# Scaled residual of two layer norms: one VectorE instruction reading PSUM in place of a TensorE product and a ScalarE copy

## The chip, the core and the metric

The kernel runs on one core of a Trainium2 chip. A core has five engines that run side by side and meet only at semaphores: TensorE (PE, matrix products into PSUM), VectorE (DVE), ScalarE (ACT), GpSimd (POOL) and SyncE (SP), which here issues loads. The metric is the device time of one execution in microseconds (us).

## What is computed

One decoder layer over 2048 tokens of width 1024. The change touches the two places at which a residual, scaled by ALPHA = 2 ** 0.25, is added ahead of a layer norm:

```python
mix = jnp.einsum('ble,ed->bld', jnp.concatenate([pool_out, attn_out], axis=-1), w_out[l])
h = layer_norm(ALPHA_RES * h + mix, ln1_g[l], ln1_b[l])
ffn = moe(h, w_router[l], b_router[l], w_gate_up[l], b_gate_up[l], w_down[l], b_down[l])
h = layer_norm(ALPHA_RES * h + ffn, ln2_g[l], ln2_b[l])
```

Everything is float32. Attention picks 256 keys per query by an index score; the mixture of experts takes the best 4 of 32 experts for every token.

## The kernel before

The tokens are cut into 16 blocks of 128. The program has five stages, one after the other: input projection (to about 600 us), attention (to about 2290 us), the placing of tokens to experts, the experts' products (to about 5607 us) and combine (to the end).

**Attention** (`attend_stage`). Each engine runs its own list of work in an order that the function `walk` writes out by hand, and the engines meet by counted semaphores. Round b of the walk handles six heads of block b, the search for the 256 best keys of block b+1 (VectorE, cut into six parts by `parts`), the index scores of block b+2 (`score`, up to four pieces), and the end of block b-1: output projection (`project`), statistics, norm, transposes, routing. The beginning of a round reads:

```python
piece("logits", b, 0)
piece("choose", b - 2)
search(b + 1, 0)
fill(b, 0, ("project", b - 1))
piece("logits", b, 1)
search(b + 1, 1)
fill(b, 1, ("score", b + 2, 0))
```

An engine skips the pieces for which it has no function. `project` on TensorE first claims the PSUM tile `pair` (two banks of 512 columns), then for each bank multiplies eight slices of `mixT` by `w_out` (L936) and adds a ninth product, `alpha_ident` (ALPHA times the identity) by `h` (L938). ScalarE's `project` copies `pair` into the tile `res` (L1039) and raises the semaphore `s_res`. VectorE's `statistics` (L776, L777), two pieces of the walk further on, waits for `s_res`; and so does TensorE's `claim` before whatever uses `pair` next: in rounds 1 to 13 that is the first product of `score(b+2, 0)` (L855), in later rounds another piece. The logits row maximum of VectorE is L756, its search rows are L725 to L730, TensorE's logits L876 and L878, its sum of the normalised diagonals L904.

**Combine** (`combine_stage`). For each block t, with two slots in turn: GpSimd makes four diagonal matrices of the gates (L1639) and gathers the rows of four experts (L1644); TensorE adds `alpha_ident` by `h1` (L1687), the gathered rows by the diagonals (L1692), in the middle of which it transposes the gate sums by expert (L1697) that VectorE made (L1716), and the bias product (L1702); ScalarE copies the sum to `total` (L1749); VectorE takes statistics (L1724 to L1729), GpSimd the power (L1651), VectorE scales (L1733, L1736), GpSimd adds the bias (L1655), ScalarE issues the store (L1753). VectorE's order within a block is gate sums, statistics, scaling. GpSimd's order is power(t), gather(t+2), bias(t). The load of `h1` for block t+1 is issued by SyncE once the product sum of block t-1 is done (`s_sum`).

Of the kernel before, what the change touches and what calls it, by code (L numbers as in the profile page):

```python
# [67 lines left out]
def wait(eng, sem, value):  # L68

    if not isinstance(value, int) or value > 0:  # L70
        eng.wait_ge(sem, value)
# [306 lines left out]
def attend_stage(nc, A, S, D_):  # L378
# [84 lines left out]
    with ExitStack() as ctx:  # L463
        def sb(name, shape, dt=F32):
            return ctx.enter_context(nc.sbuf_tensor(name, shape, dt))
# [27 lines left out]
        h1 = res  # L493
        h1T = h[:].rearrange("p (k n) -> p k n", n=P)
        ident_bf = sb("ident_bf", [P, P], BF16)
        alpha_ident = sb("alpha_ident", [P, P])
        ones = sb("ones", [P, P])
        before = sb("before", [P, P])
        expert_no = sb("expert_no", [P, EXPERTS])
# [73 lines left out]
        with nc.Block() as block:  # L573
# [57 lines left out]
            def _(pool):  # L631
# [7 lines left out]
                nc.gpsimd.iota(expert_no[:], pattern=[[1, EXPERTS]], base=0, channel_multiplier=0,  # L639
                               allow_small_or_imprecise_dtypes=True)  # L640
                nc.gpsimd.iota(token[:], pattern=[[P, TILES]], base=0, channel_multiplier=1)
                nc.gpsimd.tensor_copy(ident_bf[:], S["ident"][:])
                nc.gpsimd.tensor_scalar(alpha_ident[:], S["ident"][:], ALPHA_RES, 1.0, ALU.mult, ALU.mult
                                        ).then_inc(s_made, 1)
                pool.drain()
                pool.wait_ge(s_made, 2)
                nc.gpsimd.affine_select(out=before[:], in_=before[:], compare_op=ALU.is_gt, fill=0.0,
# [66 lines left out]
            def _(dve):  # L714
# [53 lines left out]
                def inverse(b, g):  # L768
# [2 lines left out]
                    nc.vector.reciprocal(inv_sum[:, g * REP:(g + 1) * REP], sums[:, g * REP:(g + 1) * REP]  # L771
                                         ).then_inc(s_inv, 1)

                def statistics(b):
                    dve.wait_ge(s_res, b + 1)
                    nc.vector.bn_stats(stats[:, 0:6], res[:, 0:512])  # L776
                    nc.vector.bn_stats(stats[:, 6:12], res[:, 512:1024])  # L777
                    dve.drain()
                    wait(dve, s_norm, b)
                    nc.vector.bn_aggr(mean_var, stats)  # L780
                    dve.drain()
                    nc.vector.tensor_scalar(var_eps, mean_var[:, 1:2], EPS, None, ALU.add).then_inc(s_var, 1)
# [22 lines left out]
                def weigh(b):  # L805
# [17 lines left out]
                dve.wait_ge(s_const, CONSTS)  # L823
                dve.wait_ge(s_made, 4)
                walk({"logits": logits, "inverse": inverse, "choose": choose, "search": search_part, "select": select,
                      "statistics": statistics, "weigh": weigh})

            @block.tensor
            def _(pe):
# [99 lines left out]
                def project(b, head):  # L929
                    claim(*PAIR)  # L930
                    pe.wait_ge(s_mix, KV * (b + 1))
                    pe.wait_ge(s_pools, b + 1)
                    pe.wait_ge(s_hl, 16 * (b + 1))
                    for n in range(2):
                        for k in range(KD):
                            nc.tensor.matmul(pair[:, n], mixT[:, k], w_out[:, k, n * BANK:(n + 1) * BANK],  # L936
                                             start=(k == 0), stop=False)
                        op = nc.tensor.matmul(pair[:, n], alpha_ident[:], h[:, n * BANK:(n + 1) * BANK],  # L938
                                              start=False, stop=True)
                    op.then_inc(s_out, 1)  # L940
                    used["res"] = b + 1

# [31 lines left out]
            def _(act):  # L974
# [58 lines left out]
                def project(b, head):  # L1033
                    if head:
                        exp(*head)
                    act.wait_ge(s_out, b + 1)
                    wait(act, s_h1st, 16 * b)
                    wait(act, s_ht, 2 * b)
                    nc.scalar.activation(res[:], pair[:].rearrange("p a b -> p (a b)"), ACT.Copy).then_inc(s_res, 1)  # L1039

                def norm(b):
                    act.wait_ge(s_rstd, b + 1)
# [512 lines left out]
def combine_stage(nc, A, S, D_):  # L1555


    with ExitStack() as ctx:
# [10 lines left out]
        g_now = sb("g_now", [P, TOP_E])  # L1569
        rows = sb("rows", [P, 2, TOP_E, D])  # L1570
        h1 = sb("h1_blk", [P, 2, D])
        alpha_ident = sb("alpha_ident2", [P, P])
        g_diag = sb("g_diag", [P, 2, TOP_E, P])
        by_pick = sb("by_pick", [P, TOP_E, EXPERTS])
        by_expert = sb("by_expert", [P, 2, EXPERTS])
# [36 lines left out]
        with nc.Block() as block:  # L1612
            @block.sync
            def _(sp):
                sp.dma_start(b_down[:], A["b_down"][0]).then_inc(s_const, 16)
                sp.dma_start(gain[:], A["ln2_g"][0].partition_broadcast(P)).then_inc(s_const, 16)
                sp.dma_start(bias[:], A["ln2_b"][0].partition_broadcast(P)).then_inc(s_const, 16)

                def body(t, slot, half):
                    wait(sp, s_sum, t - 1)  # L1620
                    sp.dma_start(h1[:, slot], D_["h1"][cut(t), :]).then_inc(s_h1[slot], 16)

                pairs(sp, body)

            @block.gpsimd
            def _(pool):
                nc.gpsimd.tensor_scalar(alpha_ident[:], S["ident"][:], ALPHA_RES, 1.0, ALU.mult, ALU.mult
                                        ).then_inc(s_made, 1)
                nc.gpsimd.memset(minus_half[:], -0.5).then_inc(s_made, 1)

                def gather(t, slot, half):
                    wait(pool, s_sum, t - 1)
                    if not isinstance(t, int) or t >= 2:
                        pool.wait_ge(s_rows[slot], 64 * half)
                    nc.gpsimd.tensor_copy(at[:, slot], S["pos"][:, t])
                    nc.gpsimd.tensor_copy(g_now[:], S["gates"][:, t])  # L1636
                    pool.drain()  # L1637
                    for k in range(TOP_E):
                        op = nc.gpsimd.tensor_scalar(g_diag[:, slot, k], S["ident"][:], g_now[:, k:k + 1], 1.0,  # L1639
                                                     ALU.mult, ALU.mult)  # L1640
                    op.then_inc(s_gd, 1)
                    pool.drain()  # L1642
                    for k in range(TOP_E):
                        nc.gpsimd.indirect_dma_start(  # L1644
                            rows[:, slot, k], None, D_["y"], bass.IndirectOffsetOnAxis(ap=at[:, slot, k:k + 1], axis=0)
                        ).then_inc(s_rows[slot], 16)

                def power(t, slot):
                    var_eps, rstd = small[:, slot, 14:15], small[:, slot, 15:16]
                    pool.wait_ge(s_var, t + 1)  # L1650
                    nc.gpsimd.tensor_tensor(rstd, var_eps, minus_half[:], ALU.pow).then_inc(s_rstd, 1)  # L1651

                def finish(t, slot):
                    pool.wait_ge(s_norm, t + 1)
                    nc.gpsimd.tensor_tensor(out[:, slot], out[:, slot], bias[:], ALU.add).then_inc(s_out, 1)  # L1655

                pool.wait_ge(s_made, 2)
                pool.wait_ge(s_const, 48)
                gather(0, 0, 0)
                gather(1, 1, 0)  # L1660

                def body(t, slot, half):
                    power(t, slot)
                    gather(t + 2, slot, half + 1)
                    finish(t, slot)

                for t in range(4):
                    body(t, t % 2, t // 2)
                with pool.Fori(2, TILES // 2 - 1) as i:
                    body(2 * i, 0, i)  # L1670
                    body(2 * i + 1, 1, i)
                for t in (TILES - 2, TILES - 1):
                    power(t, t % 2)
                    finish(t, t % 2)

            @block.tensor
            def _(pe):
                pe.wait_ge(s_const, 48)
                pe.wait_ge(s_made, 2)

                def body(t, slot, half):
                    pe.wait_ge(s_h1[slot], 16 * (half + 1))
                    wait(pe, s_tot, t - 1)
                    pe.wait_ge(s_gd, t + 1)
                    for n in range(2):
                        cols = slice(n * BANK, (n + 1) * BANK)
                        nc.tensor.matmul(acc[:, slot, cols], alpha_ident[:], h1[:, slot, cols], start=True, stop=False)  # L1687
                    pe.wait_ge(s_rows[slot], 64 * (half + 1))
                    for n in range(2):
                        cols = slice(n * BANK, (n + 1) * BANK)  # L1690
                        for k in range(TOP_E):
                            nc.tensor.matmul(acc[:, slot, cols], g_diag[:, slot, k], rows[:, slot, k, cols],  # L1692
                                             start=False, stop=False)
                        if n == 0:
                            pe.wait_ge(s_by, t + 1)
                            wait(pe, s_bts, t)
# [12 lines left out]
            def _(dve):  # L1709
# [9 lines left out]
                def body(t, slot, half):  # L1719
                    gates(t, slot)  # L1720
                    stats, mean_var = small[:, slot, 0:12], small[:, slot, 12:14]
                    var_eps, rstd = small[:, slot, 14:15], small[:, slot, 15:16]
                    dve.wait_ge(s_tot, t + 1)
                    nc.vector.bn_stats(stats[:, 0:6], total[:, slot, 0:512])  # L1724
                    nc.vector.bn_stats(stats[:, 6:12], total[:, slot, 512:1024])
                    dve.drain()
# [15 lines left out]
            def _(act):  # L1742
                def body(t, slot, half):
                    act.wait_ge(s_bt, t + 1)
                    wait(act, s_sum, t)
                    nc.scalar.activation(by_expertT[:], trp[0:EXPERTS, 0:P], ACT.Copy).then_inc(s_bts, 1)
                    act.wait_ge(s_sum, t + 1)
                    wait(act, s_norm, t - 1)
                    nc.scalar.activation(total[:, slot], acc[:, slot], ACT.Copy).then_inc(s_tot, 1)  # L1749

                def store(t, slot):
                    act.wait_ge(s_out, t + 1)
# [83 lines left out]
```

## Time and profile before

| | |
|---|---|
| Three runs | 5859.07, 5876.14, 5882.66 us, median 5876.14 |
| Profiled execution, its span | 5876.0 us (no other time of it is listed) |
| TensorE busy | 5062.7 us, 86% |
| VectorE busy | 3078.1 us, 52% |
| ScalarE busy | 1843.3 us, 31% |
| GpSimd busy | 977.3 us, 17% |
| Mean granted TensorE clock | 0.930 of full speed |

The span is the time from the first to the last instruction of one profiled execution. Busy shares are means over stages with different limits. A row names the line, the engine and operation, then what is written and read, with the tile's size; "idle before <- X" is the time in which the engine stood still ahead of the instruction and what ended it. "PEld" is the loading of weights, which overlaps the products.

### The profile page before, as it was taken

The numbers are of one execution on the slowest core, as the hardware profiler recorded it, in microseconds if no ns is written. First come the engines' busy times: TensorE is split into PE (matmuls) and PEld (weight loads), VectorE is DVE, ScalarE is ACT, GpSimd is POOL, SyncE is SP. The second block draws the span as 40 slices with busy tenths as digits, with TensorE's granted clock in tenths as the row PEclk, the third lists the DMA queues.
The fourth block names the chain that finished last, engine by engine and source line by source line (L and its number), as shares of the span: only waits on it lengthen the run. The fifth ranks groups of instructions, "written<-read, shape, count | busy, mean of one in ns | idle before, by whom it ended". The sixth has DMA issues, their size and how long they took to land. (4 is left out here: it accounts for less than half of the span.)

```text
span 5876.0 us, 68835 instructions
## 1 busy us (share of the span) xinstructions
PE 5062.7 (86%) x23758; PEld 3683.0 (63%) x23759; DVE 3078.1 (52%) x4877; ACT 1843.3 (31%) x2663; POOL 977.3 (17%) x1073
## 2 busy tenths in 40 slices
PE   7998788999999864889888889889888989898977
PEld 3444343444444432878887888788878878788832
DVE  2121467788777753644445444554555455544522
ACT  1111223333333321433333333333343333433310
POOL 0000122111111111211111111111111111111145
PEclk9999789999999986999999999999999999999988
DMA  5232110001000002544444543544454444544455
GB/s 189 103 115 100 45 24 17 20 16 20 12 12 10 14 8 70 184 159 152 137 160 156 170 138 130 181 138 159 164 176 138 150 167 152 183 160 137 138 178 184
DMA packets 427127, 670.22 MB, mean 114 GB/s; under 512 B 22064, under 2 KB 286256, under 8 KB 425552
## 3 DMA queue, kind: packets, MB, share of 16 engines
q1 hardware_dynamic: 367776, 507.46, 26.4%
q0 software_dynamic: 26576, 85.56, 4.1%
q10 hardware_dynamic: 32256, 69.22, 3.1%
q8 instruction: 456, 7.47, 0.5%
q14 instruction: 63, 0.52, 0.0%
HBM read 542.86 MB, written 119.31 MB: 113 GB/s over the span
## 5 line engine op out<-in xcount | busy, mean ns | idle before, releaser
L1352 PE MATMUL gu<-x_hi,w_hi 128*128 128x256 f32 (+2 forms) x4096 | 1292.6, 316 | 313.8 <-issue 218.7
L1354 PE MATMUL gu<-x_hi,w_lo 128*128 128x256 f32 (+2 forms) x4096 | 1277.6, 312 | 10.9 <-issue 10.9
L1353 PE MATMUL gu<-x_lo,w_hi 128*128 128x256 f32 (+2 forms) x4096 | 1279.0, 312 | 2.4 <-issue 2.4
L1419 DVE TENSOR_TENSOR w_lo<-w_raw,w_hi 128x2048 fp32r<-128x2048 f32 x386 | 874.7, 2287 | 529.1 <-ACT w_hi L1493 529.1
L1352 PEld LDWEIGHTS gu<-x_hi,w_hi 128*128 128x128 f32 x4096 | 820.9, 200 | 339.4 <-issue 294.5
L1493 ACT ACTIVATE w_hi<-w_raw 128x2048 fp32r<-128x2048 f32 x386 | 726.1, 1905 | 375.9 <-PE gu L1354 290.9
L1354 PEld LDWEIGHTS gu<-x_hi,w_lo 128*128 128x128 f32 x4096 | 818.4, 200 | 14.6 <-issue 14.6
L1353 PEld LDWEIGHTS gu<-x_lo,w_hi 128*128 128x128 f32 x4096 | 820.3, 200 | 0.0
L1325 POOL TENSOR_TENSOR a_lo<-up,a_hi 128x384 fp32r<-128x384 f32 x256 | 395.7, 1546 | 1965.0 <-ACT a_hi L1505 1965.0
L1430 DVE TENSOR_SCALAR gate<-gu,b_gu 128x384 f32<-128x384 f32 x256 | 158.1, 617 | 829.2 <-PE gu L1354 829.2
L1352 PE MATMUL yp<-w_hi,a_hi 128*128 128x512 f32 x1296 | 536.5, 414 | 0.0
L1353 PE MATMUL yp<-w_lo,a_hi 128*128 128x512 f32 x1296 | 523.5, 404 | 0.0
L1354 PE MATMUL yp<-w_hi,a_lo 128*128 128x512 f32 x1296 | 522.9, 403 | 0.0
L298 PE MATMUL proj_acc<-w_in_sb,hT 128*128 128x512 f32 (+1 forms) x1280 | 474.0, 531 | 7.1 <-DMA w_in_sb<-w_in 5.0
L298 PEld LDWEIGHTS proj_acc<-w_in_sb,hT 128*128 128x128 f32 x1280 | 225.3, 191 | 255.8 <-issue 249.3
L725 DVE TENSOR_SCALAR_CACHE_REDUCE mask<-scores_odd,small 128x512 bf16<-128x512 f32 (+6 forms) x224 | 346.0, 1545 | 18.7 <-issue 1.6
L1501 ACT ACTIVATE sig<-gate 128x384 f32<-128x384 f32 x256 | 132.7, 518 | 686.9 <-DVE gate L1430 686.9
L725 DVE TENSOR_SCALAR_CACHE_REDUCE mask<-scores_even,small 128x384 bf16<-128x384 f32 (+6 forms) x224 | 316.1, 1411 | 18.2 <-issue 0.7
L860 PE MATMUL acc<-relu,w_diag 128*128 128x512 f32 (+3 forms) x608 | 304.9, 600 | 0.6 <-ACT relu L983 0.3
L876 PE MATMUL qk<-kT,q_blk 128*128 128x512 f32 (+3 forms) x480 | 235.1, 574 | 79.0 <-ACT probs L998 58.4
L855 PE MATMUL pair<-ikT,iq_blk 64*128 64x512 f32 (+3 forms) x608 | 277.3, 601 | 25.1 <-ACT relu L983 23.7
L756 DVE TENSOR_REDUCE small<-qk 128x1 f32<-128x128 f32 (+15 forms) x96 | 124.0, 1291 | 324.1 <-PE qk L878 286.3
(256 smaller groups left out, 5940.2 us busy)
## 6 DMA issues: line engine op xcount, KB each, us to landing
w_raw<-w_gate_up SPq DMA_DIRECT2D x258, 1024.0 KB, 7.6
w_raw<-w_down SPq DMA_DIRECT2D x128, 1024.0 KB, 7.1
y_dram<-y_rows ACTq DMA_DIRECT2D x192, 256.0 KB, 2.9
y_dram<-zeros SPq DMA_DIRECT2D x16, 2016.0 KB
h_blk<-h_dram SPq DMA_DIRECT2D x32, 512.0 KB, 6.5
qi_dram<-qi_stage ACTq DMA_DIRECT2D x16, 640.0 KB, 2.9
w_in_sb<-w_in SPq DMA_DIRECT2D x1, 8480.0 KB, 23.7
x_in<-x SPq DMA_DIRECT2D x16, 512.0 KB, 9.2
```

Of the source, the lines that this page charges most:

```text
L298: mm = nc.tensor.matmul(acc[:, n, 0:width], hT[:, slot, k], w_in[:, k, c0:c0 + width], start=(k == 0), stop=(k == KD - 1))
L725: nc.vector.tensor_scalar(reach, s, limit, 0.0, ALU.is_ge, ALU.add, accum_out=n_reach)
L855: nc.tensor.matmul(pair[:, (u0 + i) % 2, 0:width], iq[row, b % 2, i // 2], S["ikT"][row, at:at + width], start=True, stop=True).then_inc(s ...
L860: nc.tensor.matmul(acc[:, 0:width], w_diag[:, j], relu[:, (u0 + j) % 2, 0:width], start=(j == 0), stop=(j == IDX_H - 1)).then_inc(s_wsum, 1)
L876: nc.tensor.matmul(qk[:, at:at + width], q[:, b % 2, i], S["kT"][:, i // REP, at:at + width], start=True, stop=False)
L1325: nc.gpsimd.tensor_tensor(a_lo[:, j], up[:, j % 2], a_hi[:, j].bitcast(F32), ALU.subtract).then_inc(s_al, 1)
L1352: nc.tensor.matmul(out, s_hi_, m_hi, start=(n == 0), stop=False)
L1353: nc.tensor.matmul(out, s_hi_, m_lo, start=False, stop=False)
L1354: op = nc.tensor.matmul(out, s_lo_, m_hi, start=False, stop=(n == len(pairs) - 1))
L1419: nc.vector.tensor_tensor(w_lo[:, c % 2, cols], raw[:, c % 3, cols], w_hi[:, c % 2, cols].bitcast(F32), ALU.subtract).then_inc(s_lo, 1)
L1430: nc.vector.tensor_scalar(g, gu[:, j % 2, 0, 0:ROWS], S["b_gu"][:, j, bass.ds(e, 1)], LIMIT, ALU.add, ALU.min).then_inc(s_gm, 1)
L1493: nc.scalar.activation(w_hi[:, c % 2, cols], raw[:, c % 3, cols], ACT.Copy).then_inc(s_hi, 1)
```

## The change

In attention, VectorE gets a piece `project` that computes `res = ALPHA * h + pair` in one instruction out of PSUM and raises `s_res`; the ninth product and ScalarE's copy go; the wait for `h` moves from TensorE to VectorE. In combine, VectorE computes `total = ALPHA * h1 + acc` and raises `s_tot` before it takes the statistics; the product L1687 and the copy L1749 go; SyncE's load of `h1` waits for `s_tot` in place of `s_sum`. The search parts are cut as before.

```diff
+                def residual(b, head):
+                    dve.wait_ge(s_out, b + 1)
+                    dve.wait_ge(s_hl, 16 * (b + 1))
+                    wait(dve, s_h1st, 16 * b)
+                    wait(dve, s_ht, 2 * b)
+                    nc.vector.scalar_tensor_tensor(res[:], h[:], ALPHA_RES, pair[:].rearrange("p a b -> p (a b)"),
+                                                   ALU.mult, ALU.add).then_inc(s_res, 1)
                 def statistics(b):
-                    dve.wait_ge(s_res, b + 1)
+                    dve.drain()
...
-                      "statistics": statistics, "weigh": weigh})
+                      "project": residual, "statistics": statistics, "weigh": weigh})
...
-                    pe.wait_ge(s_hl, 16 * (b + 1))
                     for n in range(2):
                         for k in range(KD):
-                            nc.tensor.matmul(pair[:, n], mixT[:, k], w_out[:, k, n * BANK:(n + 1) * BANK],
-                                             start=(k == 0), stop=False)
-                        op = nc.tensor.matmul(pair[:, n], alpha_ident[:], h[:, n * BANK:(n + 1) * BANK],
-                                              start=False, stop=True)
+                            op = nc.tensor.matmul(pair[:, n], mixT[:, k], w_out[:, k, n * BANK:(n + 1) * BANK],
+                                                  start=(k == 0), stop=(k == KD - 1))
...
-                    act.wait_ge(s_out, b + 1)
-                    wait(act, s_h1st, 16 * b)
-                    wait(act, s_ht, 2 * b)
-                    nc.scalar.activation(res[:], pair[:].rearrange("p a b -> p (a b)"), ACT.Copy).then_inc(s_res, 1)
...
-                    wait(sp, s_sum, t - 1)
+                    wait(sp, s_tot, t - 1)
...
-                    pe.wait_ge(s_h1[slot], 16 * (half + 1))
                     wait(pe, s_tot, t - 1)
                     pe.wait_ge(s_gd, t + 1)
-                    for n in range(2):
-                        cols = slice(n * BANK, (n + 1) * BANK)
-                        nc.tensor.matmul(acc[:, slot, cols], alpha_ident[:], h1[:, slot, cols], start=True, stop=False)
...
-                    dve.wait_ge(s_tot, t + 1)
+                    dve.wait_ge(s_sum, t + 1)
+                    dve.wait_ge(s_h1[slot], 16 * (half + 1))
+                    nc.vector.scalar_tensor_tensor(total[:, slot], h1[:, slot], ALPHA_RES, acc[:, slot],
+                                                   ALU.mult, ALU.add).then_inc(s_tot, 1)
+                    dve.drain()
...
-                    act.wait_ge(s_sum, t + 1)
-                    wait(act, s_norm, t - 1)
-                    nc.scalar.activation(total[:, slot], acc[:, slot], ACT.Copy).then_inc(s_tot, 1)
```

GpSimd no longer makes the two `alpha_ident` tiles.

## Rows read from the trace of the kernel before

**Rows 1.** The page: the span.

```profile
span 5876.0 us, 68835 instructions
```

**Rows 2.** Stretches by stage: busy us of PE, PEld, DVE, ACT, POOL, granted clock, DMA share, GB/s.

```profile
640.00:2330.00 1690.00, 1441.05 (x4640) 677.59 (x4638) 1225.58 (x2466) 519.15 (x1003) 285.28 (x395) 0.93 0.07 16
...
5608.00:5876.00 268.00, 191.34 (x400) 74.50 (x400) 68.45 (x128) 20.64 (x32) 143.94 (x192) 0.86 0.58 192
```

**Rows 3.** Waits in attention: who waited for whom, us in total, times, longest.

```profile
DVE small L756 <- PE qk L878: 252.4, 54, 18.4
...
PE pair L904 <- POOL r_diag L673: 40.1, 14, 9.5
```

**Rows 4.** Timeline of round 12: start us, us, engine, line, operation.

```profile
1716.25 1.89 DVE L756 TENSOR_REDUCE small<-qk 128x1 f32<-128x1664 f32 x1 [10.09 <-PE qk L878]
...
1730.70 1.02 PE L938 MATMUL pair<-h_blk,alpha_ident 128*128 128x512 f32 x2
...
1731.56 1.02 PE L876 MATMUL qk<-kT,q_blk 128*128 128x512 f32 x2
...
1735.15 1.13 PE L855 MATMUL pair<-ikT,iq_blk 64*128 64x512 f32 x4
...
1736.61 1.89 DVE L756 TENSOR_REDUCE small<-qk 128x1 f32<-128x1664 f32 x1
```

**Rows 5.** Timeline of rounds 1 and 13, the same places.

```profile
660.38 1.02 ACT L1039 ACTIVATE res<-pair 128x1024 f32<-128x1024 f32 x1 [17.05 <-PE pair L938]
661.61 1.13 PE L855 MATMUL pair<-ikT,iq_blk 64*128 64x512 f32 x4 [0.73 <-issue]
661.87 0.42 DVE L756 TENSOR_REDUCE small<-qk 128x1 f32<-128x256 f32 x1
...
1874.19 1.13 PE L855 MATMUL pair<-ikT,iq_blk 64*128 64x512 f32 x4
1874.29 2.02 DVE L756 TENSOR_REDUCE small<-qk 128x1 f32<-128x1792 f32 x1 [0.49 <-PE qk L878]
```

**Rows 6.** Groups by form: busy us, mean ns of one; VectorE, and ScalarE's and GpSimd's.

```profile
L739 DVE SCALAR_TENSOR_TENSOR scores_odd<-scores_odd,small,mask 128x1024 f32<-128x1024 f32 x1 | 1.3, 1285 | 0.1
L756 DVE TENSOR_REDUCE small<-qk 128x1 f32<-128x1024 f32 x6 | 7.3, 1225 | 8.7 <-PE qk L878 8.5
L1749 ACT ACTIVATE total<-c_acc 128x1024 f32<-128x1024 f32 x16 | 16.4, 1024 | 81.7 <-PE c_acc L1702 81.7
L1655 POOL TENSOR_TENSOR out_blk<-out_blk,bias 128x1024 f32<-128x1024 f32 x16 | 37.7, 2355 | 4.9 <-DVE out_blk L1736 4.6
```

**Rows 7.** Timeline of rounds 14 and 15.

```profile
2029.91 2.16 DVE L756 TENSOR_REDUCE small<-qk 128x1 f32<-128x1920 f32 x1
2034.34 2.08 PE L876 MATMUL qk<-kT,q_blk 128*128 128x512 f32 x2 [16.10 <-ACT probs L998]
...
2164.20 2.29 DVE L756 TENSOR_REDUCE small<-qk 128x1 f32<-128x2048 f32 x1 [15.33 <-PE qk L878]
```

**Rows 8.** Stretches at and behind gaps of TensorE, columns as in rows 2.

```profile
2041.00:2045.40 4.40, 0.00 (x0) 0.00 (x0) 4.17 (x7) 1.95 (x2) 0.23 (x1) 1.00 0.00 0
2045.40:2050.00 4.60, 4.58 (x8) 1.90 (x9) 2.33 (x4) 1.24 (x1) 2.60 (x4) 0.63 0.02 4
...
2179.70:2185.00 5.30, 5.25 (x7) 2.15 (x8) 0.00 (x0) 1.24 (x2) 3.15 (x5) 0.50 0.00 0
...
1848.00:1856.00 8.00, 6.16 (x19) 2.89 (x18) 0.92 (x1) 0.98 (x2) 2.06 (x4) 1.00 0.01 2
...
5749.70:5754.90 5.20, 5.13 (x10) 2.29 (x11) 0.00 (x0) 0.00 (x0) 3.43 (x6) 0.71 0.22 48
```

**Rows 9.** Timeline of combine.

```profile
5729.53 1.02 ACT L1749 ACTIVATE total<-c_acc 128x1024 f32<-128x1024 f32 x1 [5.16 <-PE c_acc L1702]
...
5735.98 0.28 PE L1697 MATMUL c_tr<-ident,by_expert 128*32 128x128 f32 x1 [1.22 <-DVE by_expert L1716]
...
5750.06 1.42 POOL L1639 TENSOR_SCALAR g_diag<-ident,g_now 128x128 f32<-128x128 f32 x4 [4.62 <-issue]
```

More of the change, by code:

```diff
@@ L495, in attend_stage @@
         ident_bf = sb("ident_bf", [P, P], BF16)
-        alpha_ident = sb("alpha_ident", [P, P])
         ones = sb("ones", [P, P])
@@ L641, in _ @@
                 nc.gpsimd.iota(token[:], pattern=[[P, TILES]], base=0, channel_multiplier=1)
-                nc.gpsimd.tensor_copy(ident_bf[:], S["ident"][:])
-                nc.gpsimd.tensor_scalar(alpha_ident[:], S["ident"][:], ALPHA_RES, 1.0, ALU.mult, ALU.mult
-                                        ).then_inc(s_made, 1)
+                nc.gpsimd.tensor_copy(ident_bf[:], S["ident"][:]).then_inc(s_made, 1)
                 pool.drain()
@@ L1571, in combine_stage @@
         h1 = sb("h1_blk", [P, 2, D])
-        alpha_ident = sb("alpha_ident2", [P, P])
         g_diag = sb("g_diag", [P, 2, TOP_E, P])
@@ L1626, in _ @@
             def _(pool):
-                nc.gpsimd.tensor_scalar(alpha_ident[:], S["ident"][:], ALPHA_RES, 1.0, ALU.mult, ALU.mult
-                                        ).then_inc(s_made, 1)
                 nc.gpsimd.memset(minus_half[:], -0.5).then_inc(s_made, 1)
@@ L1655, in finish @@
                     nc.gpsimd.tensor_tensor(out[:, slot], out[:, slot], bias[:], ALU.add).then_inc(s_out, 1)
-                pool.wait_ge(s_made, 2)
+                pool.wait_ge(s_made, 1)
                 pool.wait_ge(s_const, 48)
@@ L1678, in _ @@
                 pe.wait_ge(s_const, 48)
-                pe.wait_ge(s_made, 2)
                 def body(t, slot, half):
-                    pe.wait_ge(s_h1[slot], 16 * (half + 1))
                     wait(pe, s_tot, t - 1)
                     pe.wait_ge(s_gd, t + 1)
-                    for n in range(2):
-                        cols = slice(n * BANK, (n + 1) * BANK)
-                        nc.tensor.matmul(acc[:, slot, cols], alpha_ident[:], h1[:, slot, cols], start=True, stop=False)
                     pe.wait_ge(s_rows[slot], 64 * (half + 1))
@@ L1692, in body @@
                             nc.tensor.matmul(acc[:, slot, cols], g_diag[:, slot, k], rows[:, slot, k, cols],
-                                             start=False, stop=False)
+                                             start=(k == 0), stop=False)
                         if n == 0:
```

## The prediction

> **What bounds the kernel now.** I read the busy shares first, then the stretches by stage, then the waits of each changed stage, then the timeline around the changed instructions. The page gives a span of 5876.0 us [rows 1]. The stretches put the change's first half (attention, 640 to 2330 us) in a stretch with TensorE busy 1441 of 1690 us and VectorE 1226, and its second half (combine, 5608 to 5876 us) in one where no engine is busy all the time and DMA moves 192 GB/s [rows 2]. The 3278 us of expert work between them are not touched and I charge nothing there. In attention the waits say who is late: VectorE waits 252 us, in 54 waits, for TensorE's rows of logits, so TensorE is the bound and VectorE has room on average [rows 3]; ScalarE, idle 17 us before its first copy [rows 5], arrives early at the work that it gives away. The average is the trap: what counts is where VectorE is at the moment at which the new instruction stands in its queue.
>
> **Where the new instruction stands.** For round b of the walk, VectorE's order becomes logits(b,0), choose(b-2), first part of the search, *residual(b-1)*, logits(b,1). TensorE's order is logits(b,0), project(b-1), logits(b,1), score(b+2,0), and score claims the PSUM tile "pair", that is, it waits for the semaphore that ScalarE's copy raised and VectorE's sum will raise. Round 12 [rows 4]: the last alpha product begins at 1730.70, TensorE goes on with logits at 1731.56 and starts the score at 1735.15. VectorE is in its search until 1736.6 (its next row starts at 1736.61 with no idle before it), so the sum can't start before 1736.6, some 5 us after the projection is done.
>
> **Sum for rounds 1 to 13 (those with a score piece).** Let S be the start of the first score product (L855) and D the start of VectorE's second logits row (L756), which is when VectorE is free. D minus S is, round by round: 0.26, 2.08, 2.90, 2.08, 1.60, 1.03, 2.58, 0.97, 2.17, 0.19, 0.86, 1.46, -0.32 (13 rounds; the first, twelfth and last in [rows 4, 5]; in round 13 VectorE idles 0.49 before its row, so D there is 1873.87, the end of the search plus the usual 0.07). Together 17.9 us over 13 rounds. After the change the score starts at D + duration of the sum + hop to TensorE.
> - Duration: not in the trace. Nearest from below is ScalarE's 128x1024 copy out of PSUM, 1.024 us; from above the same kind of VectorE instruction with all operands in SBUF, 1.285 us; VectorE's own 1024-wide read of PSUM takes 1.225 [rows 6]. I take 1.25, nearest to the last two. An upper end far away is GpSimd's 1024-wide addition, 2.35 us, if the two should hold each other up.
> - Hop: in round 1 the copy starts at 660.38, takes 1.02, and the score, which waited for it, starts at 661.61: 0.21 us [rows 5].
> So 17.9 + 13 x 1.46 = +36.8 us. The saving on TensorE does not offset this: the two alpha products cost 0.86 us of its time each (1730.70 to 1731.56 [rows 4]), 1.72 us per block, but in these rounds they only make TensorE wait 1.72 us longer. After the score has started, everything in the round is paced by TensorE: VectorE's next logits row again begins with a wait for TensorE, and so does the first row of the next round (10.09 us in round 12 [rows 4]). So I carry the whole delay through, and VectorE's own 1.3 us are hidden in those waits.
>
> **Rounds 14 to 16.** Round 14 has no score piece; TensorE there waits 16.1 us for VectorE's logits row at 2029.91, so VectorE's 1.25 + 0.07 count: +1.3. Round 15: VectorE idles 15.3 us at that place, the sum lies in the idle time, TensorE's 1.72 come through: -1.7. Round 16 (last projection): -1.7, then 1.25 and a drain of 0.1 in place of the copy's 1.02 and its hand-over: -1.4 [rows 5, 7]. Together -1.8.
>
> **The clock.** The new wait is a gap on TensorE between the end of logits(b,1), now 1.72 earlier, and the new start of the score: 2.8 to 6.3 us, twelve of the thirteen over 3. Gaps in the trace show what follows: behind 4.4 us without a product the granted clock was 0.63 over the next 4.6 us, in another place 0.50 over 5.3 us, in combine 0.71 over 5.2 us, while around a gap of 1.84 us it stayed at 1.00 [rows 8]. The engine has two levels, 2.4 and 1.2 GHz, so these are 1.7, 2.6 and 1.5 us of work lost. The score piece is not pure TensorE time (ScalarE's part lies between its products), so I take 1.5 a round, twelve rounds: +18. Bounds: 0, if the level falls only inside the gap, and 2.6 x 13 = 34.
> The Trainium skill ("TensorE: Matmul & The Clock Gate", section "HAM oscillation — how this bites in real kernels") describes a loop whose every step waits for data between products and therefore begins every step at the lower clock. The rows agree; by the rule every round would pay, as in my sum; without it the sum would be 18 us smaller.
>
> **Combine.** The gather of one slot goes in a circle: last product of tile A (ends 5729.4), ScalarE's copy from 5729.53 to 5730.55, statistics, GpSimd's power, diagonals and four gathers, rows landed, products again at 5749.7 [rows 8, 9]. From the end of the product to the statistics it is 0.11 + 1.02 + 0.03 = 1.16 us now; after it 0.1 + 1.25 + 0.07 = 1.42 or, with the instruction at 1.285, 1.45: +0.29. The other tile, B, gets its end from VectorE's by_expert through the transpose (1.22 us idle at 5735.98 [rows 9]), which comes 0.29 later too. Seven turns, the last B tile and the last norm: 9 x 0.29 = +2.6. The alpha products (L1687, 1.7 us) lie in front of a wait for gathered rows or of that transpose; taking them away only lengthens a wait. The load of h1 is now issued after the sum, about 1.3 us later: it is wanted only by VectorE a tile later, and leaves the gather's transfers a little more room at first; at most 1.35 us of its 512 KB over 7.6 us, some 90 KB, or 0.4 us a turn. I take +2 for the stage, between -1 and +2.6 (up to +12 if tile B, too, were to start at the lower clock and it mattered; it waits for the other tile's rows 4.6 us anyway, at L1639 [rows 9]).
> GpSimd's alpha_ident in both stages (0.3 us each) lies before waits for loads: 0.
>
> **Sum.** 36.8 - 1.8 + 18 + 2 = +55 us on the profiled execution's span of 5876.0 us. No other time of that execution is given; the median of the three runs is 5876.14, so both give **5931 us**.
>
> **Rivals.**
> 1. *The wait without the clock*: as above, but the lower level falls in the gaps. For it: the gap of 1.84 us, behind which the clock stayed at 1.00. Against it: the three low rows in [rows 8]. 5876 + 37 = 5913 us.
> 2. *The delay is taken up later*: the late score shortens waits that TensorE now has for GpSimd's diagonals (40 us, 14 waits [rows 3]) or ScalarE. Only VectorE's 1.3 us x 14 would come through: 5876 + 18 + 2 = 5896. Against: what GpSimd does there comes after TensorE's own score piece, so it moves along.
> 3. *TensorE's saving comes through* (other side): if VectorE reached the sum before the projection was done and the sum ended before logits(b,1), 3.5 us in round 12, the score would start 1.72 earlier: 16 x -1.72 + 2 = -25.5, 5850 us. It decides from D at least 1.5 + 1.7 us earlier than S; only in round 15 is that so, in the other rounds D is at best 0.3 us before S. VectorE's start is tied to TensorE by the logits row of the same round, so a faster TensorE doesn't bring it there.
> 4. *The sum is dearer on VectorE*, towards 2.35 us: 1.1 x 14 more, 5948 us. Against: VectorE's reads of PSUM at the same place run at 1.2 ns an element.
>
> **Chances.** Forecast 0.62 (own range 5917 to 5948), rival 1 0.16, 2 0.09, 3 0.04, 4 0.07, the rest 0.02. Range for eight in ten: 5900 to 5955; its low end takes rival 1 with a cheaper sum (1.02 us), its high end rival 4 or a clock loss near its bound. Half a per cent, about what a measurement of this kernel tells from no change, is 29 us: faster 0.03 (rival 3 with a quick run), same 0.13 (rival 2, the rest of 3, the edge of 1), slower 0.84.
>
> **What would show it.** In the changed profile: the first L855 product of rounds 1 to 13 waits for VectorE, starting about 1.5 us after the search's last row, with gaps of 3 to 6 us (some 60 us of idle in all); the sum lasts 1.2 to 1.3 us; attention is longer by about 53 us, combine by 2, experts by nothing. Granted clock right behind those gaps: 0.5 to 0.7 for some 3 us; if 1.0, rival 1. If the gaps are there and the stage is not longer, rival 2. It is all wrong if L855 does not wait.

## The result and the profile after

The changed kernel is slower: 5963.48 us median (5955.01 to 5970.09) against 5867.6 (5855.55 to 5882.66), ratio 1.015, 95% interval 1.0124 to 1.0177. The forecast of 5931 us had the sign, but its range (5900 to 5955) ends below the time. The profiled execution spans 5953.4 us, 77.4 more than that of before; split at the first instruction of the placing stage's TensorE work (attention ends there) and at the last of the experts stage, it gives three differences, and the forecast has none of them to size:

| us | before | after | difference | forecast |
|---|---|---|---|---|
| up to the end of attention | 2294.2 | 2495.8 | +201.6 | +53 |
| placing and experts | 3312.8 | 3195.7 | -117.1 | 0 |
| combine | 269.0 | 261.9 | -7.1 | +2 |

Stretches of the changed kernel, columns as in [rows 2] (busy us of PE, PEld, DVE, ACT, POOL, granted clock, DMA share, GB/s); the line for before is the first in [rows 2], with a clock of 0.93:

```profile
640.00:2495.80 1855.80, 1580.86 (x4558) 704.39 (x4557) 1216.00 (x2446) 503.07 (x986) 286.34 (x392) 0.84 0.05 14
...
2495.80:5691.50 3195.70, 2823.83 (x17046) 2610.70 (x17046) 1682.32 (x1966) 1196.80 (x1356) 526.93 (x425) 0.95 0.48 161
5691.50:5953.40 261.90, 180.01 (x336) 70.20 (x336) 88.63 (x144) 4.48 (x17) 150.82 (x193) 0.79 0.58 197
```

TensorE is busy *more* in attention (1581 us, before 1441) although 32 products (64 records in the trace) were taken from it: it works at a lower clock. And the experts stage, whose code was not touched, has a higher clock (0.95, before 0.93) and is shorter. Round 12 of the walk, which answers to [rows 4]:

```profile
1907.97 0.22 PE L883 MATMUL qk<-mask,ident_bf 128*128 128x128 bf16 x1
1911.72 1.22 DVE L776 SCALAR_TENSOR_TENSOR res<-h_blk,pair 128x1024 f32<-128x1024 f32 x1 [0.24 <-issue]
1912.86 1.88 DVE L753 TENSOR_REDUCE small<-qk 128x1 f32<-128x1664 f32 x1
1913.15 1.80 PE L860 MATMUL pair<-ikT,iq_blk 64*128 64x512 f32 x4 [4.96 <-issue]
...
1921.57 2.07 PE L865 MATMUL acc<-relu,w_diag 128*128 128x512 f32 x2
1923.58 2.07 PE L860 MATMUL pair<-ikT,iq_blk 64*128 64x512 f32 x2
...
1935.60 2.07 PE L860 MATMUL pair<-ikT,iq_blk 64*128 64x512 f32 x2
```

The first lines are as forecast: the search ends, VectorE's sum starts, the score starts 1.43 us after the sum's start, behind a gap of 4.96 us. The later ones are not: pairs of products of the score piece take 2.07 us and not 1.12, and they still do at 1935.6, 22 us after the gap. The granted clock of this round, in the changed kernel and then in the kernel before:

```profile
1908.00:1913.00 5.00, 0.19 (x3) 0.00 (x0) 4.37 (x10) 0.00 (x0) 0.00 (x0) 1.00 0.00 0
1913.00:1940.00 27.00, 26.23 (x29) 7.00 (x30) 14.13 (x22) 5.94 (x10) 0.00 (x0) 0.51 0.00 0
1940.00:2045.00 105.00, 96.59 (x334) 45.05 (x333) 76.00 (x113) 39.87 (x76) 23.95 (x27) 0.97 0.04 14
```

```profile
1735.00:1752.20 17.20, 15.87 (x35) 4.53 (x32) 15.45 (x25) 6.80 (x12) 0.00 (x0) 1.00 0.01 1
1752.20:1855.00 102.80, 96.57 (x339) 45.87 (x340) 76.15 (x114) 38.85 (x74) 23.95 (x27) 0.98 0.04 15
```

During the gap the clock is still 1.00; then it is at the lower level (1.2 GHz) to the last products of the score piece, and comes back at 1940.8, while six full-height records of L865 run without a pause. The length of the score piece over the rounds, from the first score product to the next work on TensorE (L966, L968 after): 17.1 us in each of rounds 2 to 13 before, 28.3 to 30.7 after.

| sums over the rounds | forecast | measured |
|---|---|---|
| later start of the score (after VectorE's row of logits), rounds 1 to 13 | +36.8 | +37.9 |
| longer score piece, rounds 2 to 13 (by the clock) | +18 for all | +151.9 |
| rest of rounds 2 to 12 | 0 | +2.0 |

Round 1, which has no rank work to mark the end of the piece, comes to +15.1 in all. Rounds 14 to 16, from one projection's start to the next, come to +2.0, -2.0 and -3.8.

### The profile page after: what moved, and what is told of

Read it like the earlier page. It is cut to its first block and busy times, and to the rows that moved or that the text cites. A ratio compares the mean times of both kernels' runs of the same rounds, so it can differ in the third digit from the quotient of the medians.

```text
span 5953.4 us, 68604 instructions
## 1 busy us (share of the span) xinstructions
PE 5138.7 (86%) x23630; PEld 3661.1 (61%) x23631; DVE 3114.4 (52%) x4909; ACT 1810.8 (30%) x2631; POOL 987.0 (17%) x1071
## 5 line engine op out<-in xcount | busy, mean ns | idle before, releaser
L1350 PE MATMUL yp<-w_hi,a_hi 128*128 128x512 f32 x1296 | 524.3, 405 | 0.0
L860 PE MATMUL pair<-ikT,iq_blk 64*128 64x512 f32 (+3 forms) x608 | 359.2, 756 | 84.8 <-issue 61.5
L985 ACT ACTIVATE relu<-pair 128x512 f32<-128x512 f32 (+3 forms) x304 | 161.0, 543 | 774.7 <-PE acc L865 434.3
L865 PE MATMUL acc<-relu,w_diag 128*128 128x512 f32 (+3 forms) x608 | 386.2, 743 | 1.8 <-ACT relu L985 1.6
```

The lines of the kernel that those rows point to most:

```text
L860: nc.tensor.matmul(pair[:, (u0 + i) % 2, 0:width], iq[row, b % 2, i // 2], S["ikT"][row, at:at + width], start=True, stop=True).then_inc(s ...
L865: nc.tensor.matmul(acc[:, 0:width], w_diag[:, j], relu[:, (u0 + j) % 2, 0:width], start=(j == 0), stop=(j == IDX_H - 1)).then_inc(s_wsum, 1)
L985: nc.scalar.activation(relu[:, (u0 + i) % 2, 0:width], pair[:, (u0 + i) % 2, 0:width], ACT.Relu).then_inc(s_relu, 1)
L1350: nc.tensor.matmul(out, s_hi_, m_hi, start=(n == 0), stop=False)
```

## The experiments

Each kernel was compared with the kernel before on the same chip. Stage times are of its profiled execution.

| kernel | ratio (95%) | to the end of attention | placing and experts | combine | instruction packets |
|---|---|---|---|---|---|
| before | 1 | 2294.2 | 3312.8 | 269.0 | 456 |
| the change | 1.015 (1.0124 to 1.0177) | 2495.8 | 3195.7 | 261.9 | 425 |
| e1_attend_only | 1.016 (1.0132 to 1.0188) | 2493.9 | 3198.2 | 270.5 | 426 |
| e2_combine_only | 0.9983 (0.9968 to 0.9998) | 2301.4 | 3298.9 | 264.1 | 456 |
| e3_filler | 0.9908 (0.9876 to 0.994) | 2340.1 | 3215.3 | 261.7 | 426 |
| e4_early | 0.9777 (0.9748 to 0.9806) | 2278.1 | 3192.7 | 261.1 | 425 |
| e5_padded | 0.9984 (0.9972 to 0.9995) | 2300.6 | 3293.8 | 260.4 | 456 |
| e6_before_moved | 1.0004 (0.9993 to 1.0014) | 2311.3 | 3311.6 | 270.5 | 456 |
| e7_late_load | 0.999 (0.9976 to 1.0004) | 2291.9 | 3311.2 | 266.3 | 456 |
| e8_wake | 1.0193 (1.0161 to 1.0225) | 2425.5 | 3285.6 | 262.7 | 444 |
| e9_before_shifted | 0.9827 (0.981 to 0.9843) | 2299.4 | 3195.9 | 270.1 | 427 |
| e10_keep_products | 0.9978 (0.9963 to 0.9993) | 2289.3 | 3299.8 | 259.0 | 456 |

**Each half alone.** e1 is the change in `attend_stage` on the old `combine_stage`, e2 the other way round; the edits are the parts of the diff.

```diff
 # e1: attend_stage as changed, combine_stage as before
 # e2: combine_stage as changed, attend_stage as before
```

> Only the attention half of the change. The changed kernel's attention stage was 202 us longer, its experts stage 115 us shorter, its combine 7 us shorter. Theory A (the clock stays low): behind the new wait of 3 to 6 us TensorE runs the whole score piece at 1.2 GHz, some 11 us a round; attention here ends at about 2490 us, as in the changed kernel, and the granted clock in the score piece behind the wait is 0.50. Theory B (my forecast's, the delay and some 1.5 us of clock a round): attention +53 us. Experts: if the shorter stage comes from what stands before it in TensorE's program, it is shorter by 115 us here too; if it comes from the combine half, it is as before. With A and the first: about 5965 us.

> Only the combine half of the change. Attention as before (ends at about 2290 us). Theory (circle of the gather with a dearer VectorE part): combine +2.6 us. Rival (something in combine gets shorter that I did not see, the load of h1 behind the sum or the products that are gone): combine -7 us, as in the changed kernel. Experts as before, if its 115 us come from the program ahead of it; 115 us shorter, if not.

The attention half carries both large effects: attention to 2493.9 us and experts at 3198.2. The combine half leaves both (2301.4, 3298.9) and makes combine shorter, to 264.1; my circle of the gather had said +2.6. Each stage time is of one execution. The four kernels whose attention is that of before (before, e2, e7, e10) end it between 2289.3 and 2301.4 us, so differences of up to some 12 us in the first column are read no further.

**Is it the gap?** The score piece could be slow because VectorE now reads PSUM beside ScalarE. So the gap was filled:

```diff
+                FILL = {3: 4, 4: 6, 5: 6, 6: 6, 7: 5, 8: 5, 9: 6, 10: 4, 11: 5, 12: 3, 13: 4, 14: 5, 15: 2}
                 def score(b, c, head):
-                    claim(*PAIR)
                     claim(*ACC)
+                    if c == 0 and b >= 3:
+                        for _ in range(FILL[b]):
+                            nc.tensor.matmul(acc[:], S["ident"][:], w_out[:, 0, 0:BANK], start=True, stop=True)
+                    claim(*PAIR)
```

> The changed kernel, with 2 to 6 products of 128x512 f32 that nobody reads put into TensorE's new wait in rounds 1 to 13 (0.86 us each, so many that they fill it but don't lengthen it). The score starts when it did. Theory A (the wait lets the clock fall, and the score piece does not bring it back): the score piece runs at a granted clock of 1.00, attention is 120 to 150 us shorter than in the changed kernel, ending near 2345 us. Theory B (the score piece is slow for another reason, such as VectorE and ScalarE both reading PSUM): attention stays within 20 us of 2490 us.

Its round 12:

```profile
1776.79 4.51 PE L854 MATMUL acc<-w_out_sb,ident 128*128 128x512 f32 x10
1781.92 1.13 PE L865 MATMUL pair<-ikT,iq_blk 64*128 64x512 f32 x4 [0.62 <-issue]
1783.70 1.12 PE L865 MATMUL pair<-ikT,iq_blk 64*128 64x512 f32 x2 [0.65 <-ACT relu L990]
```

```profile
1782.00:1799.00 17.00, 15.66 (x33) 4.47 (x33) 13.90 (x22) 6.86 (x12) 0.00 (x0) 1.00 0.00 0
```

The wait for VectorE is there as in the changed kernel, but TensorE spends it on useless products, and in rounds 2 to 13 the score piece takes 17.1 us at 1.00 again. Attention ends 155.7 us earlier than in the changed kernel, a little more than the 120 to 150 given. Round 1 is the exception: there 2.06 us of idle were left behind the useless products, the clock fell 2 us into the piece, and it took 28.9 us, where it takes 16.2 before. Those 12.7 us and the late start (37.9) account for the 46 us that are left over the kernel before, with a few to spare. So the gap, by way of the clock, was the cause, not the readers of PSUM.

**Does the piece itself keep the clock down?** Here the useless products stand behind the gap and not in it:

```diff
                     claim(*PAIR)
                     claim(*ACC)
+                    if c == 0 and 3 <= b <= 15:
+                        for _ in range(6):
+                            nc.tensor.matmul(acc[:], S["ident"][:], w_out[:, 0, 0:BANK], start=True, stop=True)
```

> The changed kernel, with six products of 128x512 f32 that nobody reads put behind the wait, ahead of the score's first product, in rounds 1 to 13 (about 5.2 us of TensorE each time at 2.4 GHz, 10.3 at 1.2). Theory A (the score piece by itself, half-height products with pauses for ScalarE, does not bring the clock back, but dense full-height products do): the score piece behind them runs at 1.00, so each round pays about 7 us for the six and gets back about 10: attention 20 to 60 us shorter than in the changed kernel, 2430 to 2470 us. Rival (the clock does not come back for some other reason while VectorE and ScalarE read PSUM): the score stays at 0.50 and attention is 60 to 130 us longer.

```profile
1854.52 8.17 PE L853 MATMUL acc<-w_out_sb,ident 128*128 128x512 f32 x12 [4.97 <-issue]
1862.62 1.13 PE L863 MATMUL pair<-ikT,iq_blk 64*128 64x512 f32 x4
1864.43 1.12 PE L863 MATMUL pair<-ikT,iq_blk 64*128 64x512 f32 x2 [0.68 <-ACT relu L988]
```

```profile
1854.50:1859.50 5.00, 4.98 (x6) 2.18 (x7) 4.68 (x7) 0.00 (x0) 0.00 (x0) 0.50 0.00 0
1859.50:1864.50 5.00, 4.32 (x12) 1.48 (x10) 4.52 (x9) 0.72 (x2) 0.00 (x0) 0.94 0.00 0
1864.50:1884.00 19.50, 18.81 (x46) 6.50 (x48) 4.84 (x9) 6.54 (x13) 0.25 (x1) 1.00 0.00 1
```

The gap (4.97 us) and the fall are as in the changed kernel, but behind it stand six products of full height without a pause; the clock is back before they are through, and the score piece then runs at 1.00, in all 13 rounds. Attention is 70.3 us shorter than in the changed kernel, more than the 20 to 60 given, although TensorE was given 78 more products. So a piece that starts at the lower level does not get out of it before its own last products, and one that starts at the upper level stayed there in these rounds. Which property of the useless products brings the clock back, their height, their width or that they come without pauses, was not told apart. The Trainium skill ("TensorE: Matmul & The Clock Gate", section "HAM oscillation — how this bites in real kernels") tells of a loop that is throttled anew in every step; the changed kernel agrees, with a clock of 0.51 over 27 us behind a gap of 5, but for its loop the section counts about 1.67 us at the lower clock in each step, and here it was nearly the whole piece. The experts stage of e8 was nearly as long as before (3285.6), so its total is above the changed kernel's.

**Is it the place in VectorE's queue?** Two to five search steps were moved behind the sum:

```diff
+    MOVE = {2: 3, 3: 4, 4: 5, 5: 4, 6: 3, 7: 3, 8: 3, 9: 2, 10: 3, 11: 2, 12: 2, 13: 2, 14: 2}
...
-        return [min(BITS, round(...)) ... for i in range(HEADS)]
+        cut = [min(BITS, round(...)) ... for i in range(HEADS)]
+        cut[0] -= MOVE.get(b, 0)
+        return cut
```

> The changed kernel with 2 to 5 of VectorE's search steps in rounds 1 to 13 moved from behind logits(b,0) to behind logits(b,1), so that VectorE reaches the sum when the projection is done. Theory (the place in VectorE's queue is the cause): no wait of the score piece for the sum, clock 1.00 in it, TensorE's 1.72 us of a round come through: attention 15 to 25 us shorter than before the change, ending at 2265 to 2275 us. Rival (the moved steps make VectorE late at the next logits row, which had 2 to 5 us of room): attention 10 to 60 us longer than before.

```profile
1722.26 1.02 PE L884 MATMUL qk<-kT,q_blk 128*128 128x512 f32 x2
1724.05 1.22 DVE L779 SCALAR_TENSOR_TENSOR res<-h_blk,pair 128x1024 f32<-128x1024 f32 x1 [0.24 <-issue]
1725.85 1.13 PE L863 MATMUL pair<-ikT,iq_blk 64*128 64x512 f32 x4
1725.96 1.89 DVE L756 TENSOR_REDUCE small<-qk 128x1 f32<-128x1664 f32 x1 [0.69 <-PE qk L886]
```

The sum now lies inside TensorE's logits, the score starts without idle time ahead of it (from round 5 on; 0.1 to 0.7 us are left in rounds 2 to 4), and the piece takes 17.1 us at 1.00 in rounds 2 to 13. Attention is 16.1 us shorter than before the change and 11 us shorter than in the shortest of the four kernels with the old attention. The saving on TensorE, at 1.72 us a round, would be some 27 (an estimate); a loss of 11.2 us is seen in round 1, where 1.76 us of idle were left, the piece ran at 0.57 and took 27.4 us. The control has the moved steps without the change:

> The kernel before, with the same search steps moved as in e4_early and nothing else. Theory C: TensorE's program is the same length as before, so experts stay at about 3310 us; attention within 10 us of before, as ScalarE's copy never made the score wait; total 5865 to 5885 us. Rival (moving the steps is what made e4_early fast): attention some 15 us shorter here as well, or experts 115 us shorter, total 5740 to 5760 us.

Its total is the same as before within 0.1%. In the profiled execution, the longest of its ten (5895.0 us), attention is 17 us longer, outside the 10 us that I gave; 11.2 of them are the score piece of round 1, which starts behind the same 0.73 us of idle as before (where it took 16.2 us at 1.00) and takes 27.4:

```profile
661.50:664.50 3.00, 2.35 (x6) 0.56 (x6) 2.45 (x10) 1.08 (x2) 0.00 (x0) 0.91 0.00 0
664.50:689.00 24.50, 24.50 (x28) 6.95 (x28) 13.36 (x54) 4.04 (x8) 0.00 (x0) 0.52 0.00 0
```

So a score piece can also fall to the lower level without a long gap, and it then stays there; a single execution wins or loses 11 us by it. Moving the steps gains nothing by itself; it only makes room for the sum. With experts and combine also shorter, e4_early takes 5738.11 us and beats both kernels, by 2.2% and 3.8%; of the 144 us of its profiled execution against that of before, 120 are the experts stage, to which the next part turns.

**Where do the 117 us of the experts stage come from?** The stage goes through 32 visits of experts, and a visit is shorter by 3.7 us on average, in the changed kernel and, nearly, in e1, e3 and e4. The page's instruction queue (it brings the engines their code) differs too, first line before, second after:

```profile
q8 instruction: 456, 7.47, 0.5%
```

```profile
q8 instruction: 425, 6.96, 0.5%
```

That is 31 packets fewer, of 16.4 KB each, or about one a visit, and all 31 are missing in the experts stage (412 packets there before, 381 after). TensorE's waits in the stage (us, times, longest), before and then after:

```profile
PE gu L1352 <- issue: 218.7, 67, 12.3
PE e_tr L1343 <- issue: 55.5, 15, 4.5
PE gu L1352 <- DVE w_lo L1419: 53.8, 9, 6.4
```

```profile
PE gu L1350 <- DVE w_lo L1417: 124.3, 23, 6.4
PE gu L1350 <- issue: 115.9, 51, 6.6
PE e_tr L1341 <- issue: 22.6, 14, 1.9
```

Idle time for which the profile shows no releaser ("issue") is down by 136 us ahead of these products; about half of it comes back as waits for VectorE, and the rest of the stage's gain goes with the higher clock. The change had taken instructions off TensorE's program ahead of that stage. So they were put back, with no work worth the name:

```diff
 # e5, on e4_early
+                    pe.wait_ge(s_hl, 16 * (b + 1))
                     for n in range(2):
+                        nc.tensor.matmul(pair[:, n, 0:32], S["ident"][:], ones[:, 0:32], start=True, stop=True)
 # e9, on the kernel before
                     for n in range(2):
+                        if b < 14:
+                            nc.tensor.matmul(pair[:, n, 0:32], S["ident"][:], ones[:, 0:32], start=True, stop=True)
```

> The kernel of e4_early, with two products of 32 columns that are overwritten at once, and the wait for h, put back into TensorE's projection: TensorE's program ahead of the experts stage has as many instructions as before the change (32 products of 4 instructions). Theory C (the experts' loop is faster by 3.7 us a visit because TensorE's program ahead of it is shorter, so that its code lies elsewhere): experts back to about 3310 us, total about 5855 us. Rival D (it comes from another engine's program or from anything else in the attention half): experts stay at about 3195 us, total within 10 us of 5738 us.

> The kernel before, with 28 products of 32 columns put into the projections of blocks 0 to 13, overwritten at once; nothing of the change. The attention half took 32 products (128 instructions) and 16 waits off TensorE's program, 144 instructions, and fetched 31 packets fewer of instructions (425 against 456 packets, 6.96 against 7.47 MB, so 16.4 KB a packet); the kernel of e3_filler, 61 products or 244 instructions longer than the changed one, was nearly as fast in the experts stage. Theory G (what counts is where TensorE's loop lies against a grid of 16.4 KB, 256 instructions of 64 bytes): adding 112 instructions puts the loop where taking away 144 did; experts about 3195 to 3215 us, 425 packets, total about 5765 us. Rival (only a shorter program helps): experts at 3300 us or more, total 5870 us or more.

e5 has the 456 packets again and 3293.8 us in the stage; its whole advantage but 0.16% is gone. Of the 123 us that its profiled execution is longer than e4's, 101 are this stage; 22.5 are attention, where round 2's score piece (28.3 us at 0.58, in e4 17.1 at 1.00) and a stretch in round 10 ran at the lower clock in this one execution. e9, the kernel before with 28 useless small products and nothing else, has 427 packets, 3195.9 us in the stage, and is 1.7% faster (5771.46 us, expected 5765). So the stage's time depends on how many instructions stand ahead of TensorE's loop in the program, and this has nothing to do with the arithmetic of the change. Taking away 144 instructions and adding 112 do the same; the two differ by 256, one packet of 16.4 KB at the 64 bytes an instruction of the expectation. That the effect repeats at every such step is argued from these two. e3 (244 instructions more than the change, a little less than one step: 3215.3) and e8 (312 more: 3285.6) fit. The number of packets alone does not say it: e8 has 398 in the stage, fewer than before, and stood longer for "issue" ahead of the same products (292.6 us, before 218.7). Which fetch inside the loop TensorE stands for was not looked for, and nor was the best place.

**Combine.**

```diff
 # e7, on the kernel before
-                    wait(sp, s_sum, t - 1)
+                    wait(sp, s_tot, t - 1)
 # e10, on e2_combine_only
+                    pe.wait_ge(s_h1[slot], 16 * (half + 1))
                     wait(pe, s_tot, t - 1)
                     pe.wait_ge(s_gd, t + 1)
+                    for n in range(2):
+                        cols = slice(n * BANK, (n + 1) * BANK)
+                        nc.tensor.matmul(acc[:, slot, cols], S["ident"][:], h1[:, slot, cols], start=True, stop=True)
```

> The kernel before, with SyncE's load of h1 in combine waiting for ScalarE's copy (s_tot) in place of the product sum, 1.1 us later; nothing else. Combine took 269 us before and 261 to 264 with the combine half of the change. Theory E (the later load leaves the gather more room): combine 264 to 266 us here. Rival F (the gain comes from the alpha products that are gone, or from ScalarE's copy): combine stays at 268 to 270 us. Attention and experts as before.

> The kernel of e2_combine_only with the two products by h1 left in place (by the identity, overwritten at once by the first gathered rows), so of the combine half only VectorE's sum and the later load of h1 remain. Combine took 269 to 270.5 us with the old half, 266.3 with the later load alone, 264 to 260.4 with the new half. Theory H (TensorE's products delayed the gathered rows' first product of the second tile): combine 265 to 268 us. Rival (the rest of the gain comes from ScalarE's copy and its hand-over that are gone): 260 to 264 us. Attention and experts as before.

With the old combine half the stage took 269.0, 270.5, 270.5 and 270.1 us, with the new one 264.1, 261.9, 261.7, 261.1, 260.4 and 262.7, so some 8 us less. The later load of h1 alone gives nearly half of it (266.3, one execution, at the edge of the 264 to 266 of the theory). Taking TensorE's products away is not needed for the gain: e10 has them and takes 259.0, below the range of my theory and of the rival's too. But they are no neutral filling. The stretches of combine in e2 and e10:

```profile
5600.30:5864.40 264.10, 179.40 (x336) 70.13 (x336) 88.33 (x144) 4.48 (x17) 148.08 (x193) 0.78 0.57 195
5589.10:5848.10 259.00, 194.19 (x400) 75.41 (x400) 88.07 (x144) 4.45 (x17) 144.70 (x193) 0.88 0.58 199
```

The granted clock is 0.88 with them and 0.78 without, so what the products cost and what they may give back by the clock are mixed in this number. That leaves, for the other half of the gain, VectorE's sum in place of ScalarE's copy, or a load that is later still; which of them was not told apart.

## Why the prediction was wrong

- *VectorE reaches the sum late, and the score waits.* Right, and to size: +37.9 us over 13 rounds against 36.8, with gaps of 2.6 to 5.9 us (2.8 to 6.3 forecast). The sum takes 1.221 us (I took 1.25); it starts 0.24 us after the search's last instruction and not 0.07, and the next score product 1.43 after its start.
- *The delay is carried through.* Right: the rest of rounds 2 to 12 gave 2.0 us together. Rival 2 falls.
- *The clock, +18.* This is the step that failed: the loss was right in kind and mis-sized, 151.9 us against 18 (bound 34). I read what a gap costs from the rows behind three gaps [rows 8], which is 1.5 to 2.6 us, and all three had dense full-height products behind them. Behind the new gap stands a piece of half-height products with pauses for ScalarE, and it stayed at 1.2 GHz to its last products, in each of twelve rounds. My sum had asked how long the gap is, and not what follows it. The trace of before held a warning, 20 us of such a piece (384 columns wide) at 0.50 although TensorE was busy for 19.4 of them, in the stage's first score:

```profile
602.00:622.00 20.00, 19.43 (x29) 6.28 (x28) 0.45 (x2) 3.67 (x9) 0.00 (x0) 0.50 0.00 0
```

- *Experts, 0.* The second step that failed: a term put at nothing because its code is not touched, which measured -117 us. The work is untouched, but its place in TensorE's program is not, and nothing in my sum had a term for it. Without this windfall the range would have been missed by far: with the attention half's +202 alone the kernel would take about 6070 us, an estimate from 5867.6 + 201.6. That the time came out within 10 us of the range is luck.
- *Combine, +2.* Wrong by 9 us in sign and size. The circle with +0.29 us a turn may be there, no run shows it; the later load of h1, which I had put at 0.4 us a turn at most and left to weigh against it, is worth 2.7 us or somewhat more, and a second gain of some 4 us stays unexplained.
- *Rounds 14 to 16, +1.3, -1.7 and -1.4*: they came to +2.0, -2.0 and -3.8, the right signs and 2 us more saved in all; the difference lies in the last round, and its cause was not looked for.
- A slip: rival 4's 1.1 x 14 on top of 5931 gives 5946 us, not 5948. Nothing hangs on it; the sum took 1.22 us, so rival 4 falls.

## What to carry to other kernels

An instruction moved to another engine costs what its place in that engine's queue costs: read where that engine stands when the input is ready, and move other work behind it if it is late (the change went from +1.5% to -2.2% by that; without the windfall in the experts stage, as in e5, there is 0.2% left of it). Price a new gap on TensorE by the piece behind it, at both clock levels, and not by the gap alone. And before a whole-kernel time is taken as the worth of a small edit, split it by stages: a stage that the edit doesn't touch can move by more than the edit is worth, here 117 us by the place of a loop in the program.

## What the hardware showed that I had not expected

- A score piece of 512 columns (64-row products alternating with full ones, paused by ScalarE) that is at the lower clock stays there to its last products: 28.3 to 30.7 us at 0.51 to 0.57, against 17.1 at 1.00. Six f32 products without a pause ahead of it raised the clock in each of 13 rounds (e8). The upper level is less sure: in e6 and e3 the piece of round 1 fell 2 to 3 us after its start, and in the kernel before a narrow piece (128 columns, at 738.40) fell from 1.00 to 0.50 about 4 us in, with no pause over 0.4 us in it.
- 28 products of 32 columns, added to 23758 records on TensorE, made the kernel 1.7% faster, by the place of a later loop; with it 29 packets of instructions fewer were fetched (e9).
- VectorE's `(h * alpha) + PSUM` over 128x1024 f32 took 1.220 to 1.222 us in all 16 cases, as long as its plain read of PSUM (1.225 [rows 6]) and 0.2 longer than ScalarE's copy.
